# Attention mixers: the back-transposes of step u-2 directly behind the scores of step u

## What is computed

```python
def _token_mixers(h, w_in, ...):
    proj = h @ w_in
    a, b, c, d = jnp.split(proj, [A_COLS, A_COLS + B_COLS, A_COLS + B_COLS + C_COLS], axis=-1)
    o_a = _mixer_window(a, sink, slopes[:WIN_HEADS])
    o_b = _mixer_mla(b, mla_q_norm, mla_w_uq, mla_kv_norm, mla_w_ukv, pos)
    o_c = _mixer_axial(c, ax_q_norm, ax_k_norm)
    o_d = _mixer_diff(d, diff_lambda, diff_subln, slopes[WIN_HEADS:], layer_idx)
    return jnp.concatenate([o_a, o_b, o_c, o_d], axis=-1) @ w_out
```

## Time and profile before

| | |
|---|---|
| median of 3 runs | 3600.93 us |
| the profiled execution | 3603.71 us, span of the trace 3601.9 us |
| TensorE busy | 3386.3 us (94%) |
| DVE busy | 1855.2 us (52%) |
| ACT busy | 1419.2 us (39%) |
| mean granted TensorE clock | 0.967 of full speed |
| HBM | 284.26 MB read, 80 GB/s over the span |
| first mixer, from its first scores to its last output wait | about 1813 to 2073 us |
| second mixer | about 2905 to 3158 us |

### The profile page before, as it was taken

One profiled execution on the slowest core, in us unless ns is written; L12 is line 12 of the kernel. 1 busy time (PEld: TensorE's weight loads), 2 busy tenths in 40 slices (PEclk: granted clock), 3 DMA queues, 4 the chain that ended last, 5 costly groups with the idle time before them and its releaser, 6 DMA issues.

```text
span 3601.9 us, 46709 instructions
## 1 busy us (share of the span) xinstructions
PE 3386.3 (94%) x17244; PEld 2770.1 (77%) x17244; DVE 1855.2 (52%) x2584; ACT 1419.2 (39%) x2175; POOL 11.1 (0%) x13
## 2 busy tenths in 40 slices
PE   7988799999799999999999989999999999889997
PEld 6867688888588888888866578888888876578886
DVE  4576666636566644333567563335333467663335
ACT  3341344424644434222457543324332356642223
POOL 0000000000100000000000000000000000000000
PEclk9998899999899999999999899999999999999998
DMA  3210122322122222223211022232322210022233
GB/s 127 82 59 1 40 85 93 99 95 90 63 82 99 93 98 91 99 94 100 76 59 32 28 77 99 93 100 82 102 97 97 88 59 30 30 71 99 93 100 101
DMA packets 89734, 288.45 MB, mean 80 GB/s; under 512 B 9968, under 2 KB 14576, under 8 KB 89072
## 3 DMA queue, kind: packets, MB, share of 16 engines
q1 hardware_dynamic: 89440, 284.69, 23.9%
q0 software_dynamic: 144, 1.71, 0.1%
HBM read 284.26 MB, written 2.10 MB: 80 GB/s over the span
## 4 chain that ended last, share of the span: by engine, by line
PE 82%; DVE 9%; ACT 4%; issue 3%; DMA 1%; DVEq 0%; ACTq 0%; SPq 0%
PE gb L548 24%; PE gb L550 23%; PE gb L549 23%; PE gb L1049 2%; PE pm L1062 1%; PE pm L1082 1%; PE gb L870 1%; DVE wl L1754 1%; DMA wst<-in_weights 1%; ACT wh L1210 1%; DVE rinv L1784 1%; DVE work_a L2238 1%; PE pm L879 1%; ACT h L1260 1%; DVE h L1770 1%
## 5 line engine op out<-in xcount | busy, mean ns | idle before, releaser
L548 PE MATMUL gb<-xh,wh 128*128 128x512 f32 (+1 forms) x3264 | 1231.5, 377 | 88.8 <-DVE xl L1808 30.4
L550 PE MATMUL gb<-xh,wl 128*128 128x512 f32 (+1 forms) x3264 | 1206.8, 370 | 0.0
L549 PE MATMUL gb<-xl,wh 128*128 128x512 f32 (+1 forms) x3264 | 1206.7, 370 | 0.0
L1754 DVE TENSOR_TENSOR wl<-wst,wh 128x1024 fp32r<-128x1024 f32 (+3 forms) x600 | 645.7, 1091 | 472.4 <-ACT wh L1210 466.9
L548 PEld LDWEIGHTS gb<-xh,wh 128*128 128x128 f32 x3264 | 624.5, 191 | 233.3 <-issue 70.7
L1210 ACT CAST wh<-wst 128x1024 fp32r<-128x1024 f32 (+3 forms) x600 | 554.8, 941 | 599.4 <-DMA wst<-in_weights 599.1
L549 PEld LDWEIGHTS gb<-xl,wh 128*128 128x128 f32 x3264 | 625.9, 192 | 103.2 <-issue 5.1
L550 PEld LDWEIGHTS gb<-xh,wl 128*128 128x128 f32 x3264 | 625.2, 192 | 102.4
L548 PE MATMUL gb<-hid,wh 128*128 128x512 f32 (+2 forms) x1212 | 448.1, 370 | 9.3 <-DVE wl L1754 9.3
L550 PE MATMUL gb<-hid,wl 128*128 128x512 f32 (+2 forms) x1212 | 444.6, 367 | 0.0
L549 PE MATMUL gb<-hid,wh 128*128 128x512 f32 (+2 forms) x1212 | 444.6, 367 | 0.0
(11 more groups left out here) (360 smaller groups left out, 2988.1 us busy)
## 6 DMA issues: line engine op xcount, KB each, us to landing
wst<-in_weights SPq DMA_DIRECT2D x408, 512.0 KB, 3.3
wst<-in_weights SPq DMA_DIRECT2D x84, 384.0 KB, 2.9
wst<-in_weights SPq DMA_DIRECT2D x84, 320.0 KB, 2.9
h<-in_x_t SPq DMA_DIRECT2D x2, 1024.0 KB, 6.1
out_t<-h SPq DMA_DIRECT2D x8, 256.0 KB, 2.3
tab<-in_first SPq DMA_DIRECT2D x1, 1984.0 KB, 15.0
wst<-in_weights SPq DMA_DIRECT2D x20, 96.0 KB, 2.1
tab<-in_second POOLq DMA_DIRECT2D x1, 1666.0 KB, 7.3
```

What stands on the lines that cost most here:

```text
L548: pe.matmul(dst, w_hi, x_hi, start=start, stop=False)
L549: pe.matmul(dst, w_hi, x_lo, start=False, stop=False)
L550: return pe.matmul(dst, w_lo, x_hi, start=False, stop=stop)
L1754: dve.tensor_tensor(wl[:, s, m, a], wst[:, s, m, a], f32(wh[:, s, m, a]), ALU.subtract).then_inc(lo_split, 1)
```

## The change

In TensorE's queue of the mixer, `turn` of step u-2 moves from behind the second half of the projections and `values(u-4)` to directly behind `scores(u)`. In the turns of the loop behind step 39, where there are no scores, `turn` stands ahead of the output products. The other engines' queues are as before, and so are all waits and signals of each function.

```diff
--- before.py
+++ after.py
@@ -1153,6 +1153,9 @@
                         for c, i in projected[:ahead]:
                             part_of(c, i)
                         scores(u)
+                    if u - 2 in LAST:
+                        turn(LAST.index(u - 2))
+                    if u < NS:
                         for c, i in projected[ahead:]:
                             part_of(c, i)
                     else:
@@ -1160,8 +1163,6 @@
                             out_part(k)
                     if u - 4 in LAST:
                         values(LAST.index(u - 4))
-                    if u - 2 in LAST:
-                        turn(LAST.index(u - 2))
                     for c, i in PARTS[u] if u < NS else ():
                         if c >= 9:
                             part_of(c, i)
```

## The result

The changed kernel takes 3624.42 us (median of 4 runs, 3622.42 to 3625.55) against 3602.22 us before: the ratio is 1.0061, 95% interval 1.0044 to 1.0079, so 16 to 28 us slower. The forecast was 3615 us (3604 to 3625). Direction and range hold, the range with 0.6 us to spare; the loss is 22 us and not 14.

A forecast was written before the change was run, and what follows sets the result against it. TensorE's in-order queue was taken to bound the two mixers; new waits of 6.8 us in the first and 7.4 in the second, 14.2 together, added to the median of 3600.93 gave 3615 us, range 3604 to 3625.

The forecast's parts named there:

- both were covered by what lay between: In the old order, projections and values(u-4) covered the transposes' two inputs: DVE's normalised weights and the previous transposes' copy from PSUM.
- Seams at nothing: Changed neighbours in TensorE's queue cost 0, bounds -0.1 and +0.1 us per step, 6 us either way over both mixers.
- axial steps: Steps 18 to 24: copy done about when scores end, so counted 0; upper bound one wait of 0.7 us.
- Diff steps: Odd steps 5 to 15: new waits for DVE of 0.34, 0.66, 0.57 us in 5, 9, 13; sum 1.57 us per mixer.
- Window steps: Steps 25, 29, 33: values move behind waits for ACT's copy, plus 1.0, 0.6, 0.85; 2.45 us second mixer, 1.85 first.
- Latent steps: Steps 34 to 39: one new wait of 1.0 us in step 36, later steps don't wait; bounds 0.5 and 1.1.
- Tail: Step 40: new wait of 2.4 us per mixer for ACT's copy, output products queued behind it; bounds 1.5 and 2.6.
- Step 41 has a whole step of cover again: Tail, step 41: claimed no new wait after step 40's, the copies being ready a whole step ahead.
- Rival 1: Waits absorbed by later waits of scores for DVE; only the tail's 2 x 2.4 us remains: 3605.7 us, chance 0.15.
- 4 (ACT released earlier): ACT was late because of the transposes; moving them earlier gives back up to 13.2 us: 3588 us, chance 0.04.
- Rival 2: Clock falls behind each tail wait and one wait per mixer further up, 6.7 us more: 3622 us, chance 0.22.
- Rival 3: Clock falls less as the shift moves the low clock elsewhere; 7 us back (3608) or 14 (3601), chance 0.05.

The follow-up runs named there:

- values_first: Changed kernel, but values(u-4) go ahead of the transposes in every step (scores, values, transposes, projections): 3594.67 us, ratio to before 0.9979 to 0.9996.
- diff_only: Kernel before, with the transposes moved early only up to step 17 (differential steps): 3602.67 us, ratio to before 0.9999 to 1.0018.
- fill_middle: Kernel before, with transposes early only in steps 18 to 39 and 12 useless products added in step 27's wait: 3611.83 us, ratio 1.0015 to 1.0034.
- third_buffer: Changed kernel, but the next to last turn (30) is copied into a third SBUF buffer: 3622.10 us, ratio to before 1.0040 to 1.0065.
- tail_only: Kernel before, with the transposes early only in the four turns behind step 39: 3610.47 us, ratio to before 1.0019 to 1.0040.
- not_step9: Changed kernel, but with step 9 in the old order (transposes behind the values): 3628.41 us, ratio to before 1.0047 to 1.0075.
- latent_only: Kernel before, with the transposes early only in the latent steps 34 to 39: 3608.65 us, ratio to before 1.0010 to 1.0027.

## Why the prediction was right, and where it was off

- **Bound and direction** held. TensorE's order sets the time in the mixers, and every new wait forecast in steps 5, 9, 13, 25, 33, 36 and 40 stands in the trace. The values-first kernel, which differs from the changed one by the place of the values alone, is 30 us faster; that is the evidence for the step "both were covered by what lay between". But that the measured time lies inside the range is in part luck: 3624.42 is 0.6 us below its upper end, and terms were missed as told below.
- **Seams at nothing**: held. The axial steps 18 to 23, which have no new wait, are 0.06 and 0.05 us longer in all in the two mixers. Latent scores take 1.98 us in place of 1.88 when values lie directly before them.
- **Diff steps**: the places were right (5, 9, 13; 11 hidden, 15 none), the waits 0.44, 0.75 and 0.75 us. What failed is the term's size in the trace, 3.4 and 3.6 us for 1.57: in step 9 the transposes and projections behind the wait ran at half clock (in the first mixer 4 us of half clock stood there before as well, and 8 us now). But diff_only, 2.1 us slower (-0.4 to 6.5), gives no sign that this reaches the end in an average run, and doesn't refute the forecast's 3.1 us. The release from DVE, put at 0.07 us, measured 0.23.
- **Window steps**: 3.3 us in the second mixer and 2.2 in the first between the scores of steps 24 and 34, for 2.45 and 1.85. Step 24's 0.8 us wasn't counted (its upper bound was), step 25's was less for that. The mechanism failed in step 29, where I counted the moved values (0.6 us) and not what one longer gap does to the clock: 4.3 us in each mixer of fill_middle, and 7 us by the medians. In the changed kernel's own trace this cost doesn't show, since the clock was already low from step 27: step 29 is 0.3 us longer in the first mixer and 0.8 shorter in the second, where steps 27 and 28 are 0.5 and 1.4 longer. So the sums agree with the forecast partly by luck.
- **Latent steps**: 0.5 and 0.95 us for 1.0.
- **Tail**: the largest error that is settled, 3.85 us in each mixer for 2.4 (1.26 of it the second wait). The failing step is "Step 41 has a whole step of cover again". I had checked when the transposes could *read and write* their banks, and not when the copy behind them may overwrite its own target. `copy_turned` waits for the values of two turns before, and the change put those values behind the transposes. third_buffer, in whose traces the second wait is gone, shows it.
- **Sum**: 21.6 us in the trace less 14.2 forecast leaves 7.4. Of these 2.9 are the tail and 3.8 the differential steps; the rest is 1.2 in the window steps less 0.6 in the latent ones. By kind, the two stretches hold 15.9 us more idle time of TensorE, near the 14.2 forecast plus the 2.5 of the tail's second waits, and 5.7 us more busy time, at least in part work at half clock, which the sum put at nothing.
- **Rivals.** Rival 1 (absorbed) and 4 (ACT released earlier) are out, as the tail got longer. Rival 2 (the clock falls behind new waits) came true for one wait further up, step 9, and not for the tail: its waits of 2.38 and 2.23 us had full clock behind them in seven of the eight mixers with them (changed, tail_only, third_buffer, not_step9). The prediction's remark that the trace before shows no 2.4 us wait with products behind it is a misreading. It has a wait of 2.42 us at 1782.0 us with the clock at 0.57 over the 6 us behind it, and one of 2.63 us at 259.3 us with the clock at 1.00, so both outcomes could have been seen. Its wait of 2.71 us had half clock behind it for 8 us and not 4 (3104 to 3112). Rival 3 (the clock falls less) didn't happen in the changed kernel, whose mixers have the clock of before (0.93 and 0.96 after 0.93 and 0.97). It shows in the first mixers of diff_only, values_first and latent_only; since latent_only has the old order there, the cause may be the execution and not the order.
- **What stays open**: how much of the 22 us is waits and how much clock in an average run, and what lets the half clock last 4 us once and 24 us another time in the same steps of the same code. One profiled execution per kernel can't say, and not_step9 and latent_only warn against adding up such parts.

## What to carry to other kernels

Before moving an instruction across others in an in-order queue, list its waits *and* the waits of those who consume it, down to the buffer that each consumer overwrites: here a ring of two made the copy depend on work that the move had put behind its own producer. Put the work that is ready ahead of the instruction that waits (values, then transposes), and where an engine must idle for several microseconds anyway, look at what it runs behind that gap. Filling one 4.2 us wait with useless products gained 9 us (4 to 10), and taking 2 us of splitting out from in front of a copy gained 10 by the medians. And don't price a step by one profile: behind one and the same wait the kernel before had 24 us of half clock in its first mixer and 4 us in its second.

## What the runs showed of the hardware that was not expected

- Twelve products of 128x512 without use (3.0 us) made the kernel 4 to 10 us faster and its runs steadier (2.6 us between the fastest and the slowest, 10 us before).
- Directly behind the gap of 4.2 us in step 27 stood half clock in ten mixers of ten, and it lasted from 4 to 25 us.
- A gap of 2.10 us before the transposes of step 29 was followed by half clock in four mixers of four, one of 1.30 us in the same place in two of fourteen. A gap of 2.23 to 2.38 us in step 40 was followed by it in one of eight. So the length of the gap alone doesn't decide; what else does, no run here separates.
- The release of a TensorE wait took 0.14 us from ACT and 0.23 us from DVE's L2263.
